# Gate/up products of a Strassen-like SwiGLU FFN taken two row tiles at a time, with 1024-wide VectorE and ScalarE instructions

## The reference

```python
def swiglu(x, w_gate, w_up, w_down):
    return (jax.nn.silu(x @ w_gate) * (x @ w_up)) @ w_down

h = swiglu(rms_norm(x, g[0]), ffn_w_gate[l, 0], ffn_w_up[l, 0], ffn_w_down[l, 0])
x = x + HALF * rms_norm(h, g[1])
```

## Time and profile before

| | |
|---|---|
| three timed runs | 2664.77, 2668.12, 2668.9 us (median 2668.12) |
| profiled execution | 2661.38 us |
| its span, slowest core | 2659.8 us (cores 2649.5 to 2659.8) |
| TensorE busy | 2504.3 us, 94%, 11545 matmuls |
| VectorE busy | 1561.2 us, 59% |
| ScalarE busy | 1274.5 us, 48% |
| POOL busy | 535.7 us, 20% |
| mean granted TensorE clock | 0.983 to 0.986 |
| panels | 256 KB each from HBM, median 5.6 to 6.2 us from issue to landing |

### The profile page before, as it was taken

The page is one execution under the profiler, slowest core; times in us unless marked ns, Lnnn a source line. Parts: engine busy times, 40 slices in busy tenths (PEclk is TensorE's granted clock), DMA queues, the critical chain, the costliest instruction groups (busy, mean ns, idle before and its releaser), DMA issues.

```text
span 2659.8 us, 39099 instructions; the slowest of 8 cores (2649.5 to 2659.8 us)
## 1 busy us (share of the span) xinstructions
PE 2504.3 (94%) x11545; PEld 1132.4 (43%) x11648; DVE 1561.2 (59%) x2703; ACT 1274.5 (48%) x2150; POOL 535.7 (20%) x954
## 2 busy tenths in 40 slices
PE   6899999987999899999989999999999997998997
PEld 2344444443454344444434444444445443443443
DVE  4755763455385775576386386455537668635643
ACT  5443543437767654454354354341137775433432
POOL 1113112215120112311311221220012102122121
PEclk9999999999999999999999999999999999999998
DMA  8459958947470356985995797692246305589667
GB/s 188 74 96 163 217 89 129 186 75 138 66 126 1 87 81 96 153 203 89 142 220 88 119 197 136 101 164 62 36 68 100 60 1 127 88 125 207 114 109 151
DMA packets 164542, 310.69 MB, mean 117 GB/s; under 512 B 19184, under 2 KB 45040, under 8 KB 164336
## 3 DMA queue, kind: packets, MB, share of 16 engines
q0 software_dynamic: 132624, 229.40, 55.3%
q1 hardware_dynamic: 31712, 78.77, 9.6%
HBM read 498.64 MB, written 34.60 MB: 200 GB/s over the span
## 4 chain that ended last, share of the span: by engine, by line
PE 83%; DVE 6%; DMA 4%; issue 3%; ACT 2%; POOL 1%; SPq 1%; DVEq 0%; ACTq 0%; POOLq 0%
PE ps L336 83%; DMA slotf_55<-wflat 1%; DMA X<-xT 1%; DVE XH L799 1%; DVE X L843 1%; DMA slotf_59<-wflat 1%; POOL X L843 1%; DVE X L842 1%; DVE FE L1146 1%; DVE XN L799 0%; DVE ET_107 L1146 0%; SPq L1284 0%; DMA M_151<-memT 0%; DMA slot_48<-wflat 0%; ACT r_66 L749 0%
## 5 line engine op out<-in xcount | busy, mean ns | idle before, releaser
L814 ACT ACTIVATE X<-ps,cf_sb 128x512 f32<-128x512 f32 x128 | 87.9, 687 | 384.1 <-PE ps L336 384.1
L568 POOL DMA_DIRECT2D slotf_52<-wflat x92 | 49.3, 536 | 527.3 <-DVE SW_0_85 L959 253.7
L336 PE MATMUL ps<-XN,WQK 128*128 128x512 bf16 x502 | 123.2, 379 | 0.5
L985 ACT ACTIVATE ps<-ps 128x512 f32<-128x512 f32 x172 | 100.3, 583 | 32.1 <-PE ps L336 32.1
L792 ACT ACTIVATE XN<-X 128x512 bf16<-128x512 f32 x176 | 104.8, 628 | 21.6 <-DVE X L843 14.6
L568 POOL DMA_DIRECT2D slotf_56<-wflat x92 | 49.3, 536 | 277.0 <-DVE slotf_59 L959 146.3
L336 PE MATMUL ps<-XH,slotf_52 128*128 128x512 f16 x360 | 97.0, 384 | 6.6 <-DVE XH L799 6.6
L568 POOL DMA_DIRECT2D slotf_58<-wflat x92 | 49.3, 536 | 267.2 <-DVE slotf_53 L959 144.4
L336 PE MATMUL ps<-TX_80,SW_1_86 128*128 128x512 f16 x344 | 88.2, 379 | 13.9 <-DVE SW_1_86 L959 11.5
L568 POOL DMA_DIRECT2D slotf_54<-wflat x92 | 49.3, 536 | 252.4 <-DVE slotf_57 L959 134.6
L336 PE MATMUL ps<-TX_80,SW_1_83 128*128 128x512 f16 x344 | 90.6, 385 | 9.6 <-DVE SW_1_83 L959 5.8
(11 more groups left out here) (509 smaller groups left out, 5774.6 us busy)
## 6 DMA issues: line engine op xcount, KB each, us to landing
xscr<-X SPq DMA_DIRECT2D x48, 512.0 KB, 14.1
X<-xscr SPq DMA_DIRECT2D x48, 512.0 KB, 13.0
slotf_52<-wflat POOLq DMA_DIRECT2D x76, 256.0 KB, 5.6
slotf_53<-wflat POOLq DMA_DIRECT2D x76, 256.0 KB, 5.6
slotf_54<-wflat POOLq DMA_DIRECT2D x76, 256.0 KB, 6.0
slotf_55<-wflat POOLq DMA_DIRECT2D x76, 256.0 KB, 5.8
slotf_56<-wflat POOLq DMA_DIRECT2D x76, 256.0 KB, 5.8
slotf_57<-wflat POOLq DMA_DIRECT2D x76, 256.0 KB, 5.9
```

Of the source, the lines that this page charges most:

```text
L336: self.q["pe"].append((waits, (lambda e: e.matmul(out, lhsT=l_, rhs=r_, start=st, stop=sp, skip_group_check=grp)), inc))
L568: self.k.dma("pool", lambda e, dst=dst, src=src: e.dma_start(out=dst, in_=src), "w%d" % idx, cost=1.6, reads=([("X", c, 0) for c in range( ...
L814: k.later({"act": lambda e: e.activation(out=oap, in_=P[bank][:, :], func=AF.Copy, scale=gcol)}, reads=[("P", bank)] + CONST, writes=okeys ...
L985: k.later({"act": lambda e: e.activation(out=P[b][:, :], in_=P[a][:, :], func=AF.Copy)}, reads=[("P", a)], writes=[("P", b)])
```

## The change

Two row tiles (i stands for tiles 2i and 2i+1) are handled by one object, `Pair`, with four neighbouring panels: both gate panels, then both up panels. A product is eight matmuls, four into each bank of a pair of neighbouring banks. Every VectorE and ScalarE instruction of the gate/up stage then works on both at once, 1024 elements per partition in place of 512, and there are half as many. PSUM is declared as four tensors of two banks; `bank2` gives out such pairs, filling a bank with one matmul where a full one is asked for and there is none; `bank` prefers, in these stages, a bank whose partner is taken. The weight sums have one set of buffers for a pair in place of two sets for a tile; e2, e3 and Silu(b) share a ring of four places of 1024 fp32. The plan has two new events: "in" makes the pair and queues three of its four sums, "last" queues s4. The slot ring is aligned to 8 in front of each half in place of to 2 in front of each FFN. X, XN, XNF and XH are laid out by token pair, [2, 8, 1024] in place of [8, 2048]. Modelled costs of the wide steps are 1.03 (ScalarE), 1.23 and 0.70 (VectorE).

The diff, cut: the changes of layout that only rename an access are left out, and so is the renaming of a slot's key to a list of keys.

```diff
+    def bank2(self, full=False):
+        self.held = []
+        while True:
+            free = set(self._free())
+            ds = [d for d in range(4) if {2 * d, 2 * d + 1} <= free]
+            if ds:
+                break
+            waiting = [d for b in range(8) for d in self.pend_rw.get(("P", b), ())]
+            if waiting:
+                self._force([min(waiting, key=self.pending.index)])
+            else:
+                self._run(self._best()[1])
+        d = min(ds, key=lambda d: (full and not (self.full[2 * d] and self.full[2 * d + 1]),
+                                   self.ready("pe", [], [("P", 2 * d), ("P", 2 * d + 1)])))
+        self.reserved.update((2 * d, 2 * d + 1))
+        for b in (2 * d, 2 * d + 1):
+            if full and not self.full[b]:
+                self.fill(b)
+        return d
...
-    X = sb("X", OFF_X, [8, S], F32)
+    X = sb("X", OFF_X, [2, 8, 2 * TB], F32)
...
-    SW = [[AT(nc, "SW%d_%d" % (q, i), 90112 + (q * 3 + i) * 1024, [TB], F16) for i in range(3)] for q in range(2)]
-    ER = [AT(nc, "ER%d" % i, 96256 + i * 2048, [TB], F32) for i in range(7)]
+    ER = [AT(nc, "ER%d" % i, 90112 + i * 4096, [2, TB], F32) for i in range(3)]
+    SW = [AT(nc, "SW%d" % i, 102400 + i * 2048, [2, TB], F16) for i in range(3)]
+    SS2 = nc.alloc_sbuf_tensor_at("ss2", [128, 2, TB], F32, offset=SB_BASE + OFF_S)
...
+        class Pair:
+            def __init__(self, l, f, hf, i):
+                self.i, self.hf = i, hf
+                self.w = [ws.acquire(("gu", l, f, 2 * i + q, nm)) for nm in ("g", "u") for q in range(2)]
+                s0 = self.w[0].idx
+                gk = self.w[0].keys + self.w[1].keys
+                uk = self.w[2].keys + self.w[3].keys
+                blk = lambda r, h: SL.h[:, s0 + 2 * r:s0 + 2 * r + 2, h * TB:(h + 1) * TB]
+                (s1, q1), (s2, q2), (s4, q4) = [SW[n]((0, 2), (0, TB)) for n in (2, 0, 1)]
+                self.ops = {"P1": (blk(0, 0), gk), "P2": (blk(0, 1), gk), "P3": (s4, q4), "P4": (blk(1, 1), uk),
+                            "P5": (s1, q1), "P6": (s2, q2), "P7": (blk(1, 0), uk)}
...
+                ew(s1, blk(1, 0), blk(1, 1), ALU.add, uk, q1)
+                ew(s2, s1, blk(0, 0), ALU.subtract, q1 + gk, q2)
+                ew(blk(1, 0), blk(0, 0), blk(1, 0), ALU.subtract, gk + uk, uk)
+                self.last = lambda: ew(s4, blk(0, 1), s2, ALU.subtract, gk + q2, q4)
+
+            def prod(self, pr, d, x, first):
+                w, wk = self.ops[pr]
+                for q in range(2):
+                    pairs = [(w[:, q, kk * 128:(kk + 1) * 128], x[0](kk), wk + x[1]) for kk in range(4)]
+                    k.mm(P[2 * d + q][:, :], pairs, 2 * d + q, start=first, cont=not first)
...
                 if pr == "P1":
+                    self.a = a = k.bank2()
+                    self.prod(pr, a, blk(0, lo), True)
+                    self.b = b = k.bank2(full=True)
+                    act(PP[b][:, :, :], PP[a][:, :, :], AF.Copy, pk(a), pk(b))
                 elif pr == "P6":
+                    self.prod(pr, a, tx(1), False)
+                    self.e2, self.q2 = ering()
+                    act(self.e2, PP[a][:, :, :], AF.Copy, pk(a), self.q2)
...
                 else:
+                    self.prod(pr, c, blk(4, hi), False)
                     e2, q2, e3, q3 = self.e2, self.q2, self.e3, self.q3
+                    dve(e2, PP[c][:, :, :], e2, ALU.add, pk(c) + q2, q2, post=free(c))
+                    act(e2, e2, AF.Silu, q2, q2, func="silu")
+                    hap, hkeys = H((2 * i, 2 * i + 2), (TB, 2 * TB))
+                    dve(hap, e2, e3, ALU.mult, q2 + q3, hkeys)
...
-        PLAN = (("P1", 0), ("P6", 3), ("P5", 5), ("P7", 6), ("P2", 8), ("P4", 9), ("P3", 11))
+        PLAN = (("in", -2.5), ("P1", 0), ("last", 1.5), ("P6", 2), ("P5", 3), ("P7", 4), ("P2", 5), ("P4", 6), ("P3", 8))
 
         def ffn(l, f, n_post, nxt):
-            ws.align(2)
             for hf in range(2):
+                ws.align(8)
...
+                i0 = j0 // 2
+                ev = sorted((7 * (i - i0) + (1 if pr == "P5" and i == i0 else off), i, pr) for i in range(i0, NJ // 2) for pr, off in PLAN)
+                ps = {}
+                k.wide = True
+                for _, i, pr in ev:
+                    if pr == "in":
+                        ps[i] = Pair(l, f, hf, i)
+                    elif pr == "last":
+                        ps[i].last()
+                    else:
+                        ps[i].run(pr)
+                k.wide = False
```

More of the change, by code:

```diff
@@ L210, in __init__ @@
         self.full = [False] * 8
+        self.wide = False
         self.ws = WS(self, sched)
@@ L524, in bank @@
             self._force([min(waiting, key=self.pending.index)])
-        b = min(free, key=lambda b: (max(self.t["pe"], self.ready("pe", [], [("P", b)])), (b - self._bank) % 8))
+        b = min(free, key=lambda b: (self.wide and b ^ 1 in free, max(self.t["pe"], self.ready("pe", [], [("P", b)])),
+                                     (b - self._bank) % 8))
         self._bank = (b + 1) % 8
@@ L588, in _slot, with _at @@
     def _slot(self, pkey, pos):
-        half = pkey is not None and pkey[0] in ("gu", "d")
-        return Slot(pos, pos % NSLOT, (self.slots16 if half else self.slots)[pos % NSLOT])
+        at = self._at(pkey, pos % NSLOT)
+        return Slot(pos, pos % NSLOT, at.h, at((0, SLOT_ELEMS))[1])
+    def _at(self, pkey, idx):
+        return (self.slots16 if pkey is not None and pkey[0] in ("gu", "d") else self.slots)[idx]
     def release(self, slot):
@@ L1002, in run @@
+                    dve(e3, PP[c][:, :, :], e3, ALU.add, pk(c) + q3, q3)
                 elif pr == "P2":
                     b = self.b
[L1004 to L1007 removed]
+                    self.prod(pr, b, blk(4, lo), False)
@@ L1008, in run @@
+                    self.g, self.qg = ering()
+                    act(self.g, PP[b][:, :, :], AF.Silu, pk(b), self.qg, func="silu", post=free(b))
                 elif pr == "P4":
-                    a, s = self.a, self.r
-                    k.mm(P[a][:, :], self.wx(u.t[:, TB:2 * TB], uk, tx(2)), a, start=False, cont=True)
-                    ws.release(g)
-                    ws.release(u)
-                    hap, hkeys = H(j, (0, TB))
-                    k.later({"dve": lambda e: e.tensor_tensor(out=hap, in0=P[a][:, :], in1=SS[s][:, :], op=ALU.mult)},
-                            reads=[("P", a), ("S", s)], writes=hkeys, post=lambda: k.reserved.discard(a))
+                    a = self.a
@@ L1016, in run @@
+                    self.prod(pr, a, tx(2), False)
+                    for w in self.w:
+                        ws.release(w)
+                    hap, hkeys = H((2 * i, 2 * i + 2), (0, TB))
+                    dve(hap, PP[a][:, :, :], self.g, ALU.mult, pk(a) + self.qg, hkeys, post=free(a))
                 else:
                     c = self.c
-                    k.mm(P[c][:, :], self.wx(self.s[3][0], self.s[3][1], blk(4, (l2, h2))), c, start=False, cont=True)
+                    self.prod(pr, c, blk(4, hi), False)
```

176 lines of the change are left out of this document (78 added, 98 removed).

## The result

The changed kernel takes 1.0292 times the kernel before, 95% interval 1.0225 to 1.0360: slower, by 78 us on 2667.7. Its median over four runs, 2889.89 us, says nothing by itself, because in two of the four the cores of one die ran at a lower clock and the time rose to over 3000 us; the ratio is that of the other two, 2734.9 and 2755.6 us. Measured twice more, the same kernel stood at 1.0276 (1.0259 to 1.0292) and 1.0265 (1.0243 to 1.0288), so 1.027 or some 71 to 74 us is the better figure. The forecast was 2698, +30. The direction was right; the size was not, and the time lies above the range.

The account below looks back on a forecast made before the run. TensorE's matmuls held 83% of the span, so at most 64.6 us could be gained, at gate/up starts. Terms 17 + 35 - 15 - 8 - 1 + 2 = +30 us gave 2698 us, range 2660 to 2730.

Parts of the forecast that it names:

- Part 1, widths: Gate/up stages: 1024-wide instructions save VectorE 0.62 us per tile; nothing in middles, 8 us behind attention, 1 at first start.
- Part 2, 0.25 us per pair: Gate/up middles: TensorE stalls before P7 for ScalarE's copy of e2, queued behind a Silu; 17 us lost.
- Part 3, the direct wait: Five gate/up starts: align(8) makes panels late, 4.6 us before P1 and 2.4 before P5; 35 us lost.
- Part 3, the relief of 15: Same five starts: VectorE and ScalarE work off norms while TensorE waits, shrinking old gaps of 25.1 us by 60%, -15 us.
- Part 4, "hidden in the middles, less surely in starts": Gate/up stages: four panels released together take 9 us against 12.1 until needed; counted as nothing.
- the last rival: Gate/up starts: coarsely released panels land late in full DMA queues, 4 us in each of eight; +60, 2728, 11%.
- Heavier: Eight gate/up starts: coarse release meets spills, panels 4 us late each, norm squares delay a's copies; +60, 2728, 11%.
- The clock: Five gate/up starts: one of five panel waits brings TensorE to half clock; 2 us lost (0 to 9).

## Why the prediction missed

**Part 1, widths: right.** 0.69, 1.22, 1.01 and 1.06 us for 0.686, 1.22, 1.03 and 1.07. That the relief is worth nothing in the middles is right as well. The two gate/up stages behind attention (616 matmuls at 0.216 us each) lost 21.7 and 20.7 us on core 6, some 2 of it part 2's gaps, against 21.0 before: a relief of 1 to 2 each in place of 4.

**Part 2, 0.25 us per pair: right,** in size, place and releaser: 61 gaps of 0.25 us are 15 us, and the edit that moves the Silu took 14 off the time, where 17 were forecast.

**Part 3, the direct wait: right for P1, too large for P5.** As a mean of the cores 5.0 us ahead of P1 (4.6 forecast) and 1.1 ahead of P5 (2.4 forecast; 2.0 on core 6). The down stages, in which the first of them is counted, rose by 23 us.

**Part 3, the relief of 15: too large.** I let VectorE and ScalarE work off the norms during the wait, so that the old gaps would shrink by 15 us. Without the traffic they shrink by some 5, from 31 to 25 us, and the low clock behind the wait (+9) takes more than that; with the traffic it is not to be seen. The reading behind the term was off too: VectorE is busy 73 to 93% in these five starts by the earlier trace rows, not 85 to 90%. Even in the kernel before the alignment brought 31 us net instead of 20. A likely reason, not tested by itself, is that the wait delays the panels of the later pairs too, into the stretch in which X's exchange fills the queues, when the look-ahead that covered it is gone.

**Part 4, "hidden in the middles, less surely in starts": the step that failed.** I compared nine microseconds for four panels with the twelve until they are needed, put the term at nothing and left the rest to the last rival. Both sides of the comparison fail. The price: a panel in a full queue takes 12.1 us, as a median, and four are wanted at once; the trace before had it to read, with median landings of 7 to 12 us at 1118 to 1178, where I had taken 3.9 from a quiet stretch. The time to spare: the twelve run to the product P1, but the plan queues the sums of these panels 2.5 products sooner (4.3 us), which leaves 7.8, and VectorE stops there. 41 us hang on this step, in five stages, 8 to 9 in each. I had the place and half of the mechanism as the rival *Heavier* (4 us in each of eight stages), at +60 and 11%, with 2728 us; measured were 2735 to 2744 in most runs. The mechanism I gave there lacked its worse half: VectorE's list. A sum that waits for a late panel holds up the add and the multiply that TensorE waits for. Before, the sums waited 15.6 us in all on core 6, so nothing in that trace priced it, but the order of the list was in the code.

**The clock: under-sized.** After gaps of this length TensorE ran at 1.2 GHz for a time (PEclk 0.96, 0.90, 0.92 and 0.87 in the windows above, where the earlier trace rows has 1.00). Matmuls spaced 0.43 us instead of 0.216 cost 25 us before and 38 to 40 after, as a mean of the cores, and all of the rise is in the gate/up stages (12 before, 25 to 27 after): some 14 us for the forecast's 2. I let one of five waits bring the low clock; in the profile after, it follows the wait ahead of P1 in 39 of 40 starts (five on each core), and none of these starts has it before. It is part of the sums above, not on top.

**The Trainium skill** (SBUF — State Buffer, The DMA setup-cost knee): by its fit, an estimate of 2.6 us a panel, part 3 would have been half as long. The trace disagrees further than the forecast thought: medians of 6.9 us over the kernel and 12.1 in a start. (The 256 KB are what lands in SBUF, in fp16; from HBM twice that is read, in fp32.)

## What to carry to other kernels

A transfer's price is to be read in the stretch in which it will run: the quiet stretch gave 3.9 us, the full one 12.1, for the same 256 KB. When work is made coarser, ask what is queued on each in-order engine behind an instruction that waits for a transfer; an operand fetched early is only safe if nobody needs what stands behind it. Before a product is moved in the order, ask which copy it covered: P3's move uncovered one of 1.0 us and cost 125 us. And look-ahead thrown away in front of a burst of traffic was dear here even where nothing was wide, 31 us.

## What was not expected of the hardware

The same traffic of X, 96 transfers of 512 KB, costs one kernel nothing (0.9999 without it) and the other 39 us (1.0276 to 1.0130): here contention had no price of its own, only one by what was late behind it. A wait of some 5 us ahead of P1 brought a stretch at 1.2 GHz in 39 of 40 starts. ScalarE's and VectorE's times at width 1024 lie within 3% of a straight line between 512 and 1536 or 2048.
